# Inverse row sums by way of memory, and weight loads in ScalarE's queue, in a hybrid decoder layer

## The reference

```
mod = silu(c) @ w_ada + b_ada;  sh1, sc1, g1, sh2, sc2, g2 = split(mod, 6)
xn  = rms_norm(x, norm1_g) * (1 + sc1) + sh1
qa, ka, va, qb, kb, vb, iq, ik, iw = split(xn @ w_in)      # q, k: rms_norm per head, rotary
oa  = three dilated windows (128,1), (512,4), (2048,16), merged by their log-sum-exps   # 8 heads
I   = sum_h iw[h] * relu(iq[h] . ik);  the 256 best causal keys of each query
ob  = softmax(qb . kb over the selected keys) @ vb         # 8 query heads, 2 kv heads
x   = x + g1 * (concat(oa, ob) @ w_out)
x   = x + g2 * ((silu(gate) * up) @ w_down),  gate, up = (rms_norm(x) * (1 + sc2) + sh2) @ w_gate_up
```

## Time and profile before

| | |
|---|---|
| median of 3 runs | 1824.34 us (1822.37 to 1826.25) |
| the profiled execution | 1822.44 us |
| its span, first to last instruction | 1820.8 us |
| mean granted TensorE clock | 0.949 of full speed |
| TensorE busy | 1623.9 us (89%) |
| VectorE, ScalarE, GpSimd busy | 869.1, 680.6, 577.7 us |
| front | 0 to 545 us |
| attention of the prompt | 545 to 849 us |
| attention of the samples | 849 to 901 us |
| output projection and MLP | 901 to 1821 us |

### The profile page before, as it was taken

The page is one execution under the profiler, slowest core; times in us unless marked ns, Lnnn a source line. Parts: engine busy times, 40 slices in busy tenths (PEclk is TensorE's granted clock), DMA queues, the critical chain, the costliest instruction groups (busy, mean ns, idle before and its releaser), DMA issues.

```text
span 1820.8 us, 29717 instructions
## 1 busy us (share of the span) xinstructions
PE 1623.9 (89%) x10786; PEld 1521.4 (84%) x10786; DVE 869.1 (48%) x1998; ACT 680.6 (37%) x1777; POOL 577.7 (32%) x715
## 2 busy tenths in 40 slices
PE   4697779899947888887699889999999999999998
PEld 3595569899846777775499789999999999999998
DVE  1904777777856788886431622313303303213214
ACT  4415546757427777774222331121121111111111
POOL 2343245624644343312112052132232232232310
PEclk7798889999978999998799999999999999999999
DMA  7700014353324121102540121111111111211002
GB/s 255 249 24 6 24 40 157 100 181 100 100 64 149 59 94 47 47 8 74 211 150 17 47 70 47 47 46 46 46 46 46 46 46 35 58 46 35 12 1 96
DMA packets 138046, 135.30 MB, mean 74 GB/s; under 512 B 7229, under 2 KB 126957, under 8 KB 137302
## 3 DMA queue, kind: packets, MB, share of 16 engines
q1 hardware_dynamic: 136294, 131.07, 22.6%
q0 software_dynamic: 1648, 2.89, 0.5%
HBM read 115.29 MB, written 27.04 MB: 78 GB/s over the span
## 4 chain that ended last, share of the span: by engine, by line
PE 47%; DVE 2%; ACT 1%; DMA 1%; issue 0%; SPq 0%; DVEq 0%; ACTq 0%
PE bank L2371 27%; PE wide L2387 14%; PE bank L2350 5%; PE wide L2334 1%; DVE xn L2602 0%; DVE alo L2612 0%; DVE rstd L2586 0%; DMA out_y_p<-yn 0%; DMA ow<-in_w_out 0%; ACT ahi L2487 0%; DVE yn L2656 0%; ACT gwh L2445 0%; PE bank L2411 0%; ACT L2459 0%; ACT L2477 0%
## 5 line engine op out<-in xcount | busy, mean ns | idle before, releaser
L2623 DVE TENSOR_TENSOR hf<-bank,sg 128x352 f32<-128x352 f32 x66 | 34.6, 525 | 464.6 <-PE bank L2371 455.4
L2532 POOL TENSOR_TENSOR hlo<-hf,hhi 128x352 fp32r<-128x352 f32 x66 | 62.8, 952 | 504.8 <-ACT hhi L2461 504.8
L2371 PE MATMUL bank<-ahi,gwh 128*128 128x352 f32 x1056 | 196.4, 328 | 11.2 <-DVE hf L2623 6.6
L2636 DVE SCALAR_TENSOR_TENSOR x<-wide,modT,x 128x352 f32<-128x352 f32 (+1 forms) x264 | 151.2, 573 | 97.0 <-PE wide L2387 97.0
L2371 PE MATMUL bank<-ahi,gwl 128*128 128x352 f32 x1056 | 194.2, 326 | 0.0
L2371 PE MATMUL bank<-alo,gwh 128*128 128x352 f32 x1056 | 192.3, 324 | 2.0 <-DVE alo L2612 2.0
L2371 PEld LDWEIGHTS bank<-ahi,gwh 128*128 128x128 f32 x1056 | 176.4, 190 | 14.0 <-DVE hf L2623 6.9
L2371 PEld LDWEIGHTS bank<-alo,gwh 128*128 128x128 f32 x1056 | 174.5, 189 | 2.7 <-DVE alo L2612 2.7
L2371 PEld LDWEIGHTS bank<-ahi,gwl 128*128 128x128 f32 x1056 | 176.6, 191 | 0.0
L2387 PE MATMUL wide<-hlo,dwh 128*128 128x352 f32 x528 | 171.3, 325 | 0.0
L2387 PE MATMUL wide<-hhi,dwl 128*128 128x352 f32 x528 | 170.4, 323 | 0.0
(11 more groups left out here) (347 smaller groups left out, 3482.6 us busy)
## 6 DMA issues: line engine op xcount, KB each, us to landing
raw<-in_w_ada SPq DMA_DIRECT2D x24, 1024.0 KB, 7.5
gw<-in_w_gate_up SPq DMA_DIRECT2D x44, 512.0 KB, 4.9
raw<-in_w_in SPq DMA_DIRECT2D x11, 1024.0 KB, 5.5
dw<-in_w_down SPq DMA_DIRECT2D x22, 512.0 KB, 3.6
scr_x<-xT SPq DMA_DIRECT2D x1, 4224.0 KB, 17.9
xnat<-in_x_prompt SPq DMA_DIRECT2D x8, 512.0 KB, 5.6
scr_q<-ubuf SPq DMA_DIRECT2D x32, 128.0 KB
qn<-scr_q SPq DMA_DIRECT2D x8, 512.0 KB, 4.2
```

Of the source, the lines that this page charges most:

```text
L2371: mm = pe.matmul(pb[2 * s + side][:, 0:THIRD], a[r][:, k, side, :], b[:, k, third(th)], start=(p == 0 and k == 0), stop=(p == 2 and k == K ...
L2532: pool.tensor_tensor(hlo[:, r, third(th)], hf[:, (3 * r + th) % 2, :], hhi[:, r, third(th)].bitcast(F32), ALU.subtract).then_inc(h_lo, 1)
L2623: v.tensor_tensor(hf[:, s, :], pb[2 * s + 1][:, 0:THIRD], sg[:, s, :], ALU.mult).then_inc(h_mul, 1)
L2636: ins = v.scalar_tensor_tensor(out=x1[:, d, cols], in0=src[:, 0:n], scalar=modT[:, 40 + d, 0:1], in1=x1[:, d, cols], op0=ALU.mult, op1=ALU ...
```

## The change

Five edits; the first four are in `front`. (1) ScalarE and GpSimd split the weights of the first late chunk inside the indexer's head 2 and no longer behind it; for that `iqT` moves to the region of `ubuf`. (2) All loads from chunk 14 on are issued by ScalarE, with the same waits, at the same places in its own program. (3) So are the loads of the first attention head. (4) The page table of `attention` has a semaphore of its own. (5) In `attention` `widen`, the "r" fills and VectorE's product are gone; SP writes the reciprocals transposed to memory (`scr_r`), waits, and reads each row back into 64 partitions (`rrow`, two heads); GpSimd multiplies `oT` by it.

```
-    iqT = T.at("iqT", [P, 2, 6 * P], F32R, T.end)
+    iqT = T.at("iqT", [P, 2, 6 * P], F32R, UB)
+    EARLY_SPLIT = 2
...
 SP: for n in range(first, len(order)):
         if n in proj_no:
-            if n == first:
-                load(n + 3)
             for t in range(NTILE + 1):
                 store(proj_no[n] * (NTILE + 1) + t)
-                if t == LOAD_AT and n + 6 < len(order):
-                    load(n + 6)
-                if t == 1 and n + 1 == len(order):
-                    load_first_head()
-        elif n + 3 < len(order):
-            load(n + 3)
...
 ACT, indexer:
             for h in range(8):
                 if h + 1 < 8:
                     iq_high(h + 1)
+                if h == EARLY_SPLIT:
+                    split_w(pj[0])
...
+            def load(n):
+                kd, col, w = order[n]
+                m = n - 3
+                if m in ada_no:
+                    act.wait_ge(ada_mm, ada_no[m] + 1)
+                else:
+                    act.wait_ge(whi_done, proj_no[m] + 1)
+                    act.wait_ge(wlo_done, proj_no[m] + 1)
+                act.dma_start(raw[:, n % 3, :, 0:w], src).then_inc(raw_in[n % 3], 16)
...
-            split_w(pj[0])
...
             for n in ns:
                 if n in ada_no:
                     ada_evac(ada_no[n])
+                    if n + 3 < len(order):
+                        load(n + 3)
...
+                    if n == ns[0]:
+                        load(n + 3)
                     for t in range(NTILE + 1):
                         unit(u); root(u - 1); ...; tally_wide(q); ...
                         if t == SPLIT_AT and pj.index(n) + 1 < len(pj):
                             split_w(pj[pj.index(n) + 1])
+                        if t == LOAD_AT and n + 6 < len(order):
+                            load(n + 6)
+                        if t == 1 and n + 1 == len(order):
+                            load_first_head()
...
 POOL, indexer:
             for h in range(8):
                 pool.wait_ge(iq_hi, h + 1)
                 pool.tensor_tensor(qst[:, h % 2, :, 1, :], ...)
+                if h == EARLY_SPLIT:
+                    split_w(ns[0])
             pool.wait_ge(ik_out, 32)
             pool.wait_ge(ix_mm, 48)
-            split_w(ns[0])
...
 attention:
-    rexp = T.at("rexp", [P, 4, 2, HD], F32, T.end)
+    rrow = T.at("rrow", [P, 512], F32, T.end)
-    LAST = NSTEP + TURN + 7
+    LAST = NSTEP + TURN + 5
-    scale_at = {n + 3: u for n, u in inverse_at.items()}
...
+            def inverse_rows(u):                                   # SP
+                p, g = divmod(u, 2)
+                sp.wait_ge(inverse, u + 1)
+                for h in range(2):
+                    sp.dma_start(A["scr_r"][2 * p + h, 4 * g:4 * g + 4].rearrange("t q -> q t"),
+                                 rinv[:, 2 * p + h, 4 * g:4 * g + 4],
+                                 allow_slow_non_contiguous=True).then_inc(inverse_out, 16)
+                sp.wait_ge(inverse_out, 32 * (u + 1))
+                if u:
+                    sp.wait_ge(scaled, u)
+                for h in range(2):
+                    src = A["scr_r"][2 * p + h:2 * p + h + 1, 4 * g:4 * g + 4].rearrange("o t q -> o (t q)")
+                    sp.dma_start(rrow[HD * h:HD * h + HD, :],
+                                 src.partition_broadcast(HD).rearrange("p o n -> p (o n)")).then_inc(inverse_in, 16)
...
 SP, behind the loads of pair p:
+                if p >= 2:
+                    inverse_rows(2 * p - 4)
+                    inverse_rows(2 * p - 3)
 SP, behind the samples' loads:
+            for u in range(NH - 4, NH):
+                inverse_rows(u)
...
-            def widen(u):                                          # POOL
-                pool.wait_ge(inverse, u + 1)
-                if u:
-                    pool.wait_ge(filled, fills.index(("r", (u - 1) // 2, (u - 1) % 2)) + 1)
-                pool.tensor_copy(rexp[:], rinv[...].to_broadcast([P, 4, 2, HD])).then_inc(widened, 1)
+            def scale_rows(u):
+                p, g = divmod(u, 2)
+                pool.wait_ge(inverse_in, 32 * (u + 1))
+                pool.wait_ge(o_out, 2 * (2 * p + 1) + g + 1)
+                o = oT[:, p, 512 * g:512 * g + 512]
+                pool.tensor_tensor(o, o, rrow[:], ALU.mult).then_inc(scaled, 1)
             for h in range(1, NH):
                 highs(h)
                 lows(h)
                 if h >= 3 and h % 2:
-                    widen(h - 3)
-                    widen(h - 2)
+                    scale_rows(h - 3)
+                    scale_rows(h - 2)
                 high_v(h)
                 low_v(h)
...
-                elif kind == "r":                                  # PE
-                    pe.wait_ge(widened, 2 * a + b + 1)
-                    for j in range(4):
-                        mm = pe.transpose(dst[:, j * P:(j + 1) * P], rexp[:, j]..., ident[:])
-                elif kind == "r":                                  # DVE
-                    v.wait_ge(filled, x + 1)
-                    v.wait_ge(o_out, 2 * (2 * a + 1) + b + 1)
-                    v.tensor_tensor(o, o, src[:], ALU.mult).then_inc(dve_out, 1)
```

More of the change, by code:

```diff
@@ L269, in front @@
     qst = T.at("qst", [P, 2, 6, 2, HD], F32R, T.end)
-    iqT = T.at("iqT", [P, 2, 6 * P], F32R, T.end)
-    assert T.end <= UB
+    assert T.end <= WB + 24 * KD * P
+    iqT = T.at("iqT", [P, 2, 6 * P], F32R, UB)
+    assert T.end <= LB
     pg = T.at("pg", [P, NSEQ, 2, HD], F32, WB + 24 * KD * P)
@@ L515, in store @@
                     sp.dma_start(s[0], src).then_inc(unit_st[u % 4], 16)
[L517 to L527, removed]
             load(0)
@@ L942, in _ @@
             n = 0
+            pj = [n for n in range(ada_at + 3, len(order)) if n not in ada_no]
             for h in range(8):
@@ L954, in _, with load_first_head @@
                         copy_out(7 + 2 * h)
+            def load(n):
[6 more added lines that the diff above has]
+                    act.wait_ge(wlo_done, proj_no[m] + 1)
+                src = A["w_ada" if kd == "ada" else "w_in"][0, :, col:col + w].rearrange("(k p) n -> p k n", p=P)
+                act.dma_start(raw[:, n % 3, :, 0:w], src).then_inc(raw_in[n % 3], 16)
+            def load_first_head():
+                for r in range(4):
+                    act.wait_ge(unit_st[r], 16 * max(nst[u] for u in range(NIDX, NIDX + 3 * (NTILE + 1)) if u % 4 == r))
+                act.wait_ge(whi_done, len(proj))
+                act.wait_ge(wlo_done, len(proj))
+                act.wait_ge(ada_mm, len(adas))
+                act.dma_start(S["qn"][0][:], A["scr_q"][0:SEQ, 0:P].rearrange("(t p) c -> p t c", p=P)
+                             ).then_inc(S["q_in"][0], 16)
+                act.dma_start(S["kn"][0][:], A["win_k_p"][0, 0, :, 0:2, :].rearrange("(t p) h d -> p t (h d)", p=P)
+                             ).then_inc(S["kv_in"][0], 16)
+                act.dma_start(S["mask_a"][:], A["mask_a"]).then_inc(S["mask_in"], 16)
             def tally_wide(q):
@@ L960, in tally_wide @@
                 last.then_inc(wide_tally, 1)
-            pj = [n for n in range(ada_at + 3, len(order)) if n not in ada_no]
-            split_w(pj[0])
             def sample_relu():
@@ L1084, in _ @@
             pool.dma_start(A["ik_s"][0].rearrange("n t d -> (n t) d"), ikn[0:NSAMP, NTILE, :]).then_inc(ik_out, 16)
+            ns = [n for n in range(ada_at + 3, len(order)) if n not in ada_no]
             for h in range(8):
@@ L1089, in _ @@
                                    qst[:, h % 2, :, 0, :].bitcast(F32), ALU.subtract).then_inc(iq_lo, 1)
+                if h == EARLY_SPLIT:
+                    split_w(ns[0])
             pool.wait_ge(ik_out, 32)
-            ns = [n for n in range(ada_at + 3, len(order)) if n not in ada_no]
             pool.wait_ge(ix_mm, 48)
-            split_w(ns[0])
             for q, n in enumerate(ns):
@@ L1539, in attention @@
             fills.append(f)
-        if n in scale_at:
-            at_step[n].append(len(fills))
-            fills.append(("r", scale_at[n] // 2, scale_at[n] % 2))
     def by_act(f):
-        return f[0] == "p" or f[0] != "r" and f[2] == 0
+        return f[0] == "p" or f[2] == 0
     def by_dve(f):
-        return f[0] in ("p", "r") or f[2] == 1
+        return f[0] == "p" or f[2] == 1
     act_before = [sum(by_act(f) for f in fills[:x]) for x in range(len(fills) + 1)]
     dve_before = [sum(by_dve(f) for f in fills[:x]) for x in range(len(fills) + 1)]
-    head_fills = {h: [x for x, f in enumerate(fills) if f[0] not in ("p", "r") and f[1] == h] for h in range(NH)}
+    head_fills = {h: [x for x, f in enumerate(fills) if f[0] != "p" and f[1] == h] for h in range(NH)}
     step_fills = {m: [x for x, f in enumerate(fills) if f[0] == "p" and f[1] == m] for m in range(NSTEP)}
@@ L1597, in attention @@
     inverse = sem("row_inverse")
-    widened = sem("inverse_widened")
+    inverse_out = sem("inverse_written")
```

(10 more changed lines are left out.)

10 lines of the change are left out of this document (4 added, 6 removed).

## The result

The changed kernel takes 1877.2 us (median, 1876.06 to 1884.49) against 1823.4 for the kernel before: ratio 1.0308, interval 1.0277 to 1.0338. It is 54 us slower, where 21 us faster was forecast, and outside the range of 1793 to 1826. The profiled execution has a span of 1875.2 us.

What follows compares the result with a forecast made beforehand. Bounds: TensorE in the projections, late top-k search, engines handing on in turn in attention, plus TensorE's waits. Sum -2.6 - 12.9 + 3.0 - 4.2 - 11.2 + 2.6 + 4.2 = -21.1: 1801.3 us profiled, 1803.2 against the median; range 1793 to 1826.

Steps and rivals of the forecast that it cites:

- D: Attention loop: scaling leaves TensorE and VectorE, -11.2 us; round trip through memory 7.8 us (bounds 6 and 14), costing +2.6.
- the sign of being wrong: Attention: the prediction is wrong if GpSimd's product comes over 11 us after the reciprocal.
- The +2.6 at head 11's queries: Attention: page loads busy GpSimd in head 10, so the longer round trip delays the next queries, +2.6 us (0 to +9).
- The threshold of about 10.7 us: Attention loop, first pair: a round trip up to about 10.7 us costs nothing at the next head's queries.
- Rival 3: Attention: round trip of 20 us, stalls at five pairs and 12 us at the end, +64, 1867 us; chance 0.07.
- D's removal: Attention loop: transposes and VectorE's product go, 1.6 us for each of seven pairs, -11.2 (bounds -9.7 and -12.5).
- E: End of attention loop: round trip and product with nothing beside them, +4.2 us (+2 to +11).
- A: Front: first late split moves into the indexer, 6.77 and 2.4 us saved, 6.6 added, net -2.6.
- B: Front: weight loads on ScalarE's queue shrink gaps at projection starts, -12.9 us; ScalarE's new wait at second ada chunk, +3.0.
- Rival 1: Front: stores stay late, gaps at projection starts remain; total -6.5, 1818 us; chance 0.22.
- C: End of front: first attention head's loads issued earlier, on ScalarE, so the store lands sooner, -4.2 us (-2.5 to -5).
- rival 4: Whole kernel: round trip of 6 us, gaps and clock come back wholly, 1795 us; chance 0.08.

Runs made afterwards that it cites:

- e4: The changed kernel with each write of inverse row sums in 128 pieces of 16 bytes, rows scaled by other rows' sums: 1809.6 us, ratio 0.9923 to the kernel before.
- e5: The changed kernel with each write of inverse row sums in 256 pieces of 8 bytes, rows scaled by other rows' sums: 1814.7 us, ratio 0.9952 to the kernel before.
- e6: The changed kernel with writes in their own order (16-byte pieces) and GpSimd's product reading the rows with a stride: 1809.0 us, ratio 0.9922 to the kernel before.
- e3: The changed kernel without any scaling by the inverse row sums (no round trip, no product), attention rows not normalized: 1803.0 us, ratio 0.9885 to the kernel before.
- e9: The kernel before with only the early split of the first late chunk's weights, inside the indexer: ratio 0.9986.
- e10: The kernel before with only the late chunks' weight loads moved to ScalarE's queue, the first head's loads staying on SP: ratio 0.9972.
- e11: The kernel before with only the first attention head's loads on ScalarE's queue, issued after the last project's second unit: ratio 0.9971.

## Why the prediction was wrong, by its steps

**D, the round trip, is the step that failed.** "Two issues 0.8, landing 3, two issues 0.8, landing 3, semaphores 0.2: 7.8, bounds 6 and 14": measured 14.7 at the first pair, 16.8 for its second, and past 11 us, which the prediction had named as the sign of being wrong. With 16-byte pieces it is 5.7 (e4), so all but the write's landing was sized well; the read is much longer only where slow writes follow it (up to 8.6 us). The +2.6 at head 11's queries fits too: its wait is 1.9 us in e4 and 3.8 in e5. The write's landing, 3 us in the sum, took some 10. The 3.2 us behind it were read from a store of 1024 pieces of 256 B, and a count of pieces was carried over as if their size were nothing. No row of before had a piece of 4 bytes; the upper bound, 14, came from no row and was too low. The Trainium skill's DMA: Bandwidth & Descriptors (Rules for kernel authors) had said to put the last dimension in order, one descriptor per element otherwise; e4 to e6 agree, with 68 us. The Trainium skill's price of some 10.5 ns a packet (the same page, Measured) gave me an estimate of 0.7 us, with which I had brushed the rule aside. As time of the DMA engines the trace agrees: the 1024 pieces pass in 1.1 us at a share of 0.46, which is 7.9 ns of an engine for each. As the time until the write is complete it fails: the 9.1 us come behind the last packet.

**D again, the second product.** I let the queries wait for one round trip. Both run one after the other on SP and through one buffer, so the second had 16.8 us, and it is the one that the next queries stand behind. The threshold of about 10.7 us and GpSimd's order were right: 16.8 less 10.7 is 6.1, and TensorE waited 6.94 there. **Rival 3** ("the round trip is 20 us", 1867) named this mechanism, place and size, with a chance of 0.07. It had the stall at five pairs and 12 us at the end; it came at six, with 18 at the end, and the rival left out the lower clock between the waits (13 us). The stated range left this rival out.

**D's removal** was right: -10.6 in the loop of e3, forecast -11.2. **E**, the end of the loop, fell with D's round trip: some 9 us from the last reciprocal were forecast, 22.5 measured, against 4.5 before; with e4's trip of 5.6 us it is 8.6.

**A** was right in size (-2.6 forecast, -2.6 by e9's times, -1.8 in its profile), though the detour through the indexer costs 8.6 us of TensorE's start for 6.6. Two us of it I had not seen: of VectorE's accumulations in the indexer, the longest of which was 1.36 us, one now takes 4.59, beside GpSimd's low weights.

```profile
174.43 6.79 DVE L1256 SCALAR_TENSOR_TENSOR sco<-relu,iw,sco 128x384 f32<-128x384 f32 x3 [1.31 <-ACT relu L936]
```

```profile
174.09 4.51 POOL L1030 TENSOR_TENSOR wlo<-raw,whi 128x2048 fp32r<-128x2048 f32 x1 [7.09 <-ACT whi L825]
```

The Trainium skill's SBUF — State Buffer (Who interferes with whom) tells of a port pair that GpSimd and a VectorE instruction with two SBUF inputs hold in turn, each for its whole length; this pair of rows agrees, and no run here separates it from another cause.

**B** was half right: the +3.0 at the ada chunk is there (14.47 for 11.34 us), but the gaps gave back some 6 for 12.9. "With loads in another queue the store lands in 2 to 4 us" is the sentence that failed: it took 6.2 us in e10 for 8.0 before. The gap at 330 fell to 2.4 from 4.6, but those at 362 and 482 are 3.1 and 3.4 for 3.4 and 3.6. Rival 1 ("the stores stay late") came nearer. **C** was right in the changed kernel, where 16.28 became 11.93; alone, in e11's profile, it is 13.42. Two small slips change nothing: ScalarE issues 25 DMAs, not 23, and rival 4's terms add up to 1796.

## What to carry to other kernels

Before a wait on a DMA is put into an engine's order, count its pieces and their bytes, both: two writes of 2 KB in 4-byte pieces came back after 8 to 11 us, in 16-byte pieces mostly after 2 to 3. If a layout must turn, turn it in the operand of the engine that reads it. And see what stands behind the wait in that engine's queue, taking the last of several serial trips: the same slow write cost 43 us less with the products one head later.

## What the runs showed that I had not expected

Two writes of 2 KB from SBUF to memory, waited for, take as little as 1.9 us with their issues. In 4-byte pieces they take 8.4 to 11.4 us, though the DMA engines are through with all 1024 pieces in 1.1 us: the wait of 9.1 us behind the last packet appears in no engine's busy share. A read issued just ahead of such writes can land late too, in up to 8.6 us. GpSimd's product with an operand at a stride of four elements takes 1.55 us for 1.29.
